# Two attention products cut to 64 and 32 rows of the array: one transpose fewer per head, a second bank for half of the result

## What is computed

```python
def nsa_attend(q, gates, ...):          # 8 query heads, 2 key/value groups
    s = jnp.einsum('bgrtd,bgnd->bgrtn', q, kc) * scale          # 15 compressed blocks
    p_cmp = masked_softmax(s, kc_end[None, :] <= q_pos[:, None])
    o_cmp = jnp.einsum('bgrtn,bgnd->bgrtd', p_cmp, vc)
    ...                                                         # o_sel, o_win in the same way
    return gates[..., 0:1] * o_cmp + gates[..., 1:2] * o_sel + gates[..., 2:3] * o_win
```

## Time and profile before

| what | value |
|---|---|
| runs | 1112.6, 1112.62, 1114.02 us |
| median | 1112.62 us |
| span of the profiled execution, first to last instruction | 1110.9 us |
| PE busy | 1100.0 us (99%) |
| DVE busy | 606.3 us (55%) |
| ACT busy | 419.5 us (38%) |
| mean granted TensorE clock | 0.996 of full speed |

### The profile page before, as it was taken

The page is one execution under the profiler, slowest core; times in us unless marked ns, Lnnn a source line. Parts: engine busy times, 40 slices in busy tenths (PEclk is TensorE's granted clock), DMA queues, the critical chain, the costliest instruction groups (busy, mean ns, idle before and its releaser), DMA issues.

```text
span 1110.9 us, 19312 instructions
## 1 busy us (share of the span) xinstructions
PE 1100.0 (99%) x8020; PEld 1077.8 (97%) x8020; DVE 606.3 (55%) x884; ACT 419.5 (38%) x566; POOL 66.8 (6%) x121
## 2 busy tenths in 40 slices
PE   9999999999999999999999999999999999999996
PEld 7998999999999999999999999999999999999996
DVE  6794443536456667664454467455455454454445
ACT  6733322424335444443333344333333333333332
POOL 0014000000000000001100000000000000002220
PEclk9999999999999999999999999999999999999998
DMA  8556685544444232358888744544544444464342
GB/s 297 196 189 201 228 279 189 179 152 152 168 147 173 83 113 110 114 171 295 288 277 306 257 149 171 171 171 171 171 167 153 168 145 144 147 242 146 148 150 95
DMA packets 64081, 202.03 MB, mean 182 GB/s; under 512 B 6647, under 2 KB 35607, under 8 KB 45831
## 3 DMA queue, kind: packets, MB, share of 16 engines
q1 hardware_dynamic: 58888, 185.68, 48.8%
q0 software_dynamic: 2400, 10.89, 2.8%
q10 hardware_dynamic: 2718, 4.41, 1.1%
HBM read 193.61 MB, written 11.53 MB: 185 GB/s over the span
## 4 chain that ended last, share of the span: by engine, by line
PE 99%; DVE 1%; issue 0%; DVEq 0%
PE bank L1327 27%; PE bank L1328 27%; PE bank L1329 27%; PE bank L1679 1%; PE bank L1360 1%; PE bank L1455 1%; PE bank L1450 1%; PE bank L1429 1%; PE bank L1428 1%; PE bank L1427 1%; PE bank L1594 1%; PE bank L1517 0%; PE bank L1452 0%; PE bank L1685 0%; PE bank L1345 0%; PE bank L1454 0%
## 5 line engine op out<-in xcount | busy, mean ns | idle before, releaser
L536 ACT ACTIVATE w_hi<-raw 128x2048 fp32r<-128x2048 f32 x140 | 268.1, 1915 | 572.2 <-PE bank L1329 479.9
L1327 PE MATMUL bank<-h_hi,w_hi 128*128 128x320 f32 x1536 | 479.7, 312 | 0.0
L1329 PE MATMUL bank<-h_hi,w_lo 128*128 128x320 f32 x1536 | 474.6, 309 | 0.0
L1328 PE MATMUL bank<-h_lo,w_hi 128*128 128x320 f32 x1536 | 474.5, 309 | 0.0
L814 DVE TENSOR_TENSOR w_lo<-raw,w_hi 128x2048 fp32r<-128x2048 f32 x140 | 325.2, 2323 | 186.4 <-ACT w_hi L536 186.2
L1327 PEld LDWEIGHTS bank<-h_hi,w_hi 128*128 128x128 f32 x1536 | 288.4, 188 | 3.9 <-issue 3.5
L1328 PEld LDWEIGHTS bank<-h_lo,w_hi 128*128 128x128 f32 x1536 | 288.5, 188 | 0.4
L1329 PEld LDWEIGHTS bank<-h_hi,w_lo 128*128 128x128 f32 x1536 | 288.4, 188 | 0.0
L1328 PE MATMUL bank<-oz_lo,w_hi 128*128 128x320 f32 x256 | 78.9, 308 | 0.0
L1329 PE MATMUL bank<-oz_hi,w_lo 128*128 128x320 f32 x256 | 78.8, 308 | 0.0
L1327 PE MATMUL bank<-oz_hi,w_hi 128*128 128x320 f32 x256 | 78.8, 308 | 0.0
(11 more groups left out here) (347 smaller groups left out, 1127.5 us busy)
## 6 DMA issues: line engine op xcount, KB each, us to landing
raw<-in_stream SPq DMA_DIRECT2D x140, 1024.0 KB, 5.0
cmp_t<-in_cmp_pages SPq DMA_DIRECT2D x32, 128.0 KB, 4.2
kt_moba<-in_moba_k SPq DMA_DIRECT2D x16, 256.0 KB, 3.6
kt_mem<-in_mem_k SPq DMA_DIRECT2D x8, 512.0 KB, 6.3
vs_moba<-in_moba_v SPq DMA_DIRECT2D x16, 256.0 KB
vs_mem<-in_mem_v SPq DMA_DIRECT2D x8, 512.0 KB
out_win_old<-in_cache_win POOLq DMA_DIRECT2D x8, 512.0 KB, 3.7
raw<-in_stream SPq DMA_DIRECT2D x10, 256.0 KB, 9.9
```

The costliest lines, as they stand in the source:

```text
L536: nc.scalar.activation(w_hi[:, u], raw[:, u], ACT.Copy).then_inc(hi_ready[u], 1)
L1327: nc.tensor.matmul(out[:, 0:n], w_hi[:, u, kb, :], hi[:, kb, :], start=(kb == first), stop=False)
L1328: nc.tensor.matmul(out[:, 0:n], w_hi[:, u, kb, :], lo[:, kb, :], start=False, stop=False)
L1329: mm = nc.tensor.matmul(out[:, 0:n], w_lo[:, u, kb, :], hi[:, kb, :], start=False, stop=(kb == last))
```

## The change

For the prompt: the compressed probabilities of both halves stand side by side in one block `p_c` of 128 columns (the first half in columns 0 to 14, the second in columns 32 to 46), which is transposed once. Of the transposed block rows 0 to 31 and 32 to 63 are multiplied apart, each with a copy of the compressed values on the same rows of `vc_g`: the first half goes on into bank OB, the second into bank P1, which is free after its transposed probabilities are copied out. DVE adds P1 to `o_t` (`compressed_added`, semaphore `c_added`), and TensorE waits for that before it writes P1 again. Two copies of the compressed values are computed per group instead of one.

For the samples: of `vs_new` only rows 0 to 63 are used in the first half of the product and only rows 96 to 127 in the second; the second half of the result goes to bank S2 instead of the second half of OB, and DVE copies the two banks in two instructions.

```diff
-        p_c = at("p_c", [P, 2, P], f32, Z_ + 15 * 4 * TOK)
+        p_c = at("p_c", [P, P], f32, Z_ + 15 * 4 * TOK)
+        p_cq = p_c[:, 0:64].rearrange("p (q n) -> p q n", q=2)
...
                 if i % REP == 0:
-                    nc.vector.tensor_copy(vc_g[0:N_CMP, :], S1[0:N_CMP, 384:512]).then_inc(vc_rdy, 1)
+                    for r in range(0, 64, 32):
+                        nc.vector.tensor_copy(vc_g[r:r + N_CMP, :], S1[r:r + N_CMP, 384:512]).then_inc(vc_rdy, 1)
...
+            def compressed_added(i):
+                dve.wait_ge(o_copied, i + 1)
+                slot = o_t[:, i, P:SEQ]
+                nc.vector.tensor_tensor(slot, slot, P1[:, 0:P], ALU.add).then_inc(c_added, 1)
...
                 z_gated(0, i)
+                compressed_added(i)
                 z_scaled(1, i)
...
-                nc.vector.tensor_copy(o_rows[:].rearrange("p n c -> p (n c)"), OB[:, 0:2 * P]).then_inc(brow_copied, 1)
+                nc.vector.tensor_copy(o_rows[:, 0, :], OB[:, 0:P])
+                nc.vector.tensor_copy(o_rows[:, 1, :], S2[:, 0:P]).then_inc(brow_copied, 1)
...
                 if i % REP == 0:
-                    mm = nc.tensor.matmul(S1[0:N_CMP, 384:512], hid[:, 1, (2 * DEC_BATCH + g) * N_CMP:(2 * DEC_BATCH + g + 1) * N_CMP],
-                                          w_phi2[:, 1, :], start=True, stop=True)
+                    for r in range(0, 64, 32):
+                        mm = nc.tensor.matmul(S1[r:r + N_CMP, 384:512], hid[:, 1, (2 * DEC_BATCH + g) * N_CMP:(2 * DEC_BATCH + g + 1) * N_CMP],
+                                              w_phi2[:, 1, :], start=True, stop=True)
...
-                    nc.tensor.transpose(bk[:, 384:512], p_c[:, n, :], ident[:])
+                    if n:
+                        pe.wait_ge(c_added, i)
+                    if n == 0:
+                        nc.tensor.transpose(bk[:, 384:512], p_c[:], ident[:])
...
-                nc.tensor.matmul(OB[:, 0:SEQ].rearrange("p (q c) -> p q c", q=2), vc_g[:], pt_c, start=False, stop=True)
+                for q in range(2):
+                    rows = slice(32 * q, 32 * q + 32)
+                    nc.tensor.matmul((OB[:, 0:P], P1[:, 0:P])[q], vc_g[rows, :], pt_c[rows, :], start=(q == 1), stop=True)
...
+                for n, r in enumerate(quarter):
+                    nc.tensor.matmul(OB[r, 0:P], ptb_nsa[0:64, 2, r], vs_new[0:64, n * P:(n + 1) * P], start=False, stop=True)
+                for n, r in enumerate(quarter):
+                    nc.tensor.matmul(S2[r, 0:P], ptb_nsa[96:P, 2, r], vs_new[96:P, (4 + n) * P:(5 + n) * P], start=True, stop=False)
```

More of the change, by code:

```diff
@@ L250, in build @@
         (s_ready, vc_rdy, max_rdy, exp_done, p_ready, pt_ready, pt_copied, o_ready, o_copied, z_rdy, z_tanh, z_done, g0_rdy,
-         smp_saved, pt_win_copied) = [sem(n) for n in ("s_ready vc_rdy max_rdy exp_done p_ready pt_ready pt_copied o_ready "
-                                        "o_copied z_rdy z_tanh z_done g0_rdy smp_saved pt_win_copied").split()]
+         smp_saved, pt_win_copied, c_added) = [sem(n) for n in ("s_ready vc_rdy max_rdy exp_done p_ready pt_ready pt_copied o_ready "
+                                        "o_copied z_rdy z_tanh z_done g0_rdy smp_saved pt_win_copied c_added").split()]
         (b_staged, kt_in, vs_in, bs_ready, vcs_ready, vcs_copied, vcs_wr, bmax_rdy, bexp_done, bp_ready, bpt_ready, bpt_copied, brow_ready,
@@ L699, in prompt_exps @@
                 for q in range(2):
-                    softmax_rows(p_c[:, q, 0:N_CMP], q, nmx[:, q:q + 1])
+                    softmax_rows(p_cq[:, q, 0:N_CMP], q, nmx[:, q:q + 1])
                 act.wait_ge(max_rdy, i * 4 + 2)
@@ L731, in _ @@
                 act.wait_ge(pt_ready, i * 3 + 2)
-                nc.scalar.activation(pt_ab[:, 1, :], P1[:], ACT.Copy).then_inc(pt_win_copied, 1)
+                nc.scalar.activation(pt_ab[:, 1, 0:384], P1[:, 0:384], ACT.Copy).then_inc(pt_win_copied, 1)
                 z_tanh_tile(0, i)
@@ L1044, in prompt_softmax @@
                 dve.wait_ge(s_ready, i * 3 + 1)
-                nc.vector.tensor_tensor(p_c[:, 0, 0:N_CMP], S0[:, 0:N_CMP], mask_cmp[:, 0, 0:N_CMP], ALU.add)
-                ch.link(nc.vector.tensor_tensor(p_c[:, 1, 0:N_CMP], S0[:, 384 + N_CMP:384 + 2 * N_CMP], mask_cmp[:, 1, 0:N_CMP], ALU.add))
-                nc.vector.reduce_max(nmx[:, 0:2], p_c[:, :, 0:N_CMP], AX, negate=True).then_inc(max_rdy, 1)
+                nc.vector.tensor_tensor(p_cq[:, 0, 0:N_CMP], S0[:, 0:N_CMP], mask_cmp[:, 0, 0:N_CMP], ALU.add)
+                ch.link(nc.vector.tensor_tensor(p_cq[:, 1, 0:N_CMP], S0[:, 384 + N_CMP:384 + 2 * N_CMP], mask_cmp[:, 1, 0:N_CMP], ALU.add))
+                nc.vector.reduce_max(nmx[:, 0:2], p_cq[:, :, 0:N_CMP], AX, negate=True).then_inc(max_rdy, 1)
                 ch.link(nc.vector.scalar_tensor_tensor(p_sel[:], dist[:, 128:512], slope, S0[:, N_CMP:384 + N_CMP], ALU.mult, ALU.add))
@@ L1074, in scale_p @@
                                                    ALU.mult, ALU.mult)
-                scale_p(p_c[:, 0, 0:N_CMP], 0, 0, 0)
-                scale_p(p_c[:, 1, 0:N_CMP], 1, 1, 0)
+                scale_p(p_cq[:, 0, 0:N_CMP], 0, 0, 0)
+                scale_p(p_cq[:, 1, 0:N_CMP], 1, 1, 0)
                 scale_p(p_sel[:, 0:128], 2, 0, 1)
@@ L1192, in oz_split @@
                                                 ALU.subtract).then_inc(oz_lo_rdy, 1)
-            dve.wait_ge(o_copied, NSA_H)
+            dve.wait_ge(c_added, NSA_H)
             dve.wait_ge(bo_copied, 3 * DEC_BATCH)
@@ L1534, in prompt_values @@
                 pe.wait_ge(pt_win_copied, i + 1)
-                pe.wait_ge(vc_rdy, g + 1)
+                pe.wait_ge(vc_rdy, 2 * g + 2)
                 pe.wait_ge(o_copied, i)
-                pt_sel, pt_win, pt_c = pt_ab[:, 0, :], pt_ab[:, 1, :], pt_ab[:, :, 384:512]
+                pt_sel, pt_win, pt_c = pt_ab[:, 0, :], pt_ab[:, 1, :], pt_ab[:, 0, 384:512]
                 nc.tensor.matmul(OB[:, 0:SEQ], v_rows[:, 0, g * P:(g + 1) * P], pt_sel[:, 0:SEQ], start=True, stop=False)
@@ L1576, in sample_turn @@
                     nc.tensor.transpose(P0[:, m * P:(m + 1) * P], pb[:, m * P:(m + 1) * P], ident[:])
+                if b == 0:
+                    pe.wait_ge(c_added, NSA_H)
                 pe.wait_ge(bp_ready, b * 2 + 2)
@@ L1589, in sample_values @@
                 quarter = [slice(32 * n, 32 * n + 32) for n in range(4)]
-                for m in range(3):
+                for m in range(2):
                     for n, r in enumerate(quarter):
                         vs = (vs_sel, vs_win)[n // 2]
[L1593 to L1600, removed]
+                        nc.tensor.matmul(OB[r, 0:P], ptb_nsa[:, m, r], vs[:, m, n % 2 * P:n % 2 * P + P], start=(m == 0), stop=False)
+                for n, r in enumerate(quarter):
+                    nc.tensor.matmul(OB[r, 0:P], ptb_nsa[0:64, 2, r], vs_new[0:64, n * P:(n + 1) * P], start=False, stop=True)
+                for n, r in enumerate(quarter):
+                    nc.tensor.matmul(S2[r, 0:P], ptb_nsa[96:P, 2, r], vs_new[96:P, (4 + n) * P:(5 + n) * P], start=True, stop=False)
                 for m in range(2):
                     for n, r in enumerate(quarter):
-                        mm = nc.tensor.matmul(OB[r, P:2 * P], ptb_mem[:, m, r], vs_mem[:, m, n * P:(n + 1) * P], start=False, stop=(m == 1))
+                        nc.tensor.matmul(S2[r, 0:P], ptb_moba[:, m, r], vs_moba[:, m, n * P:(n + 1) * P], start=False, stop=False)
+                for m in range(2):
+                    for n, r in enumerate(quarter):
+                        mm = nc.tensor.matmul(S2[r, 0:P], ptb_mem[:, m, r], vs_mem[:, m, n * P:(n + 1) * P], start=False, stop=(m == 1))
                 mm.then_inc(brow_ready, 1)
```

## The result

The changed kernel takes 1117.22 us (median of 5 runs, 1116.8 to 1117.68) against 1112.66 us before (5 runs): ratio 1.0036, 95% interval 1.0025 to 1.0047. It is slower by some 0.4%, above the range of the forecast, which ended at 1116.1. The difference of the two medians is 4.6 us. In later runs, made beside the experiments, before had medians of 1113.5 (19 runs) and 1113.4 us (21 runs), and against these the changed kernel stands 3.7 to 3.8 us higher; the traces say 3.8 us, as follows.

The account below looks back on a forecast made before the run. TensorE, busy 99% and never waiting, was taken as the bound; -0.87 (transposes) - 1.7 (pair) + 1.6 (prompt shape changes) + 0 + 2.4 (sample shape changes) = +1.4 us gave 1114.0 us, range 1109.7 to 1116.1.

Parts of the forecast that it names:

- What bounds the kernel: Whole kernel: TensorE, busy 99%, never waits, so an edit is worth what it adds to or takes from its stream.
- The transposes and the pair: Prompt: 8 of 16 transposes of `p_c` go, -0.87 us; two 32-row products with `vc_g` run together, -1.7 us.
- Rival (c): Prompt: the two 32-row products do not run together, since their 128-column loads follow one another; +3.2 us, 1115.8 us, chance 0.18.
- The price of a change of shape: TensorE: 0.10 us each, 16 in the prompt for +1.6 us, 24 in the samples for +2.4 us.
- (d): Prompt and samples: a change of shape costs 0.13 us instead of 0.10, over 40 changes; +2.6 us, 1115.2 us, chance 0.06.
- the uncovered load of 128 columns: Prompt: upper bound for a change of shape, up to some 0.2 us each if the load stands uncovered; 0.10 was taken.
- Rival (a): Prompt and samples: changes of rows are free; -2.6 us, chance 0.16, or -4.4 us with sample groups together, chance 0.08.
- The 64- and the 32-row groups: Samples: the two groups on `vs_new` do not run together, being of different shapes; no gain taken, bound below -1.8 us.
- Rival (b): Samples: 64- and 32-row groups run together without a change between them, -0.2 us; with the prompt -1.2 us, 1111.4 us, chance 0.12.
- VectorE, the waits, the copies: VectorE's addition, TensorE's wait for `c_added` and the copy of `o_rows` in two pieces are all covered: 0 us.
- The sign forecast for PEld: Weight loads: PEld should show idle time put down to "issue" at each change of shape.

Follow-up runs that it names:

- `prompt_rows_32`: Kernel before, its product of 256 columns with `vc_g` summing over rows 0 to 31 instead of 128, in shape 32x128: 1116.65 us (one run).
- `one_group_64`: Kernel before, the first sample group on `vs_new` summing over rows 0 to 63 instead of 128, in shape 64x32: 1115.53 us (one run).
- `sample_64_64`: Kernel before with only the sample part changed, second group on `vs_new` on rows 64 to 127 instead of 96 to 127: 1114.12 us (one run).
- `best`: Kernel before with one transpose per head, full-row `vc_g` products, and both `vs_new` groups in 64x32 first in `sample_values`: 1111.9 against 1113.39 us, ratio 0.9988.

## Why the prediction was wrong

**What bounds the kernel: right.** TensorE is busy 99%, no new wait of it appears, and every microsecond of the loss is a longer step in its stream.

**The transposes and the pair: right.** The transposes gave 0.11 us per head. The two products of 32 rows run together, as the forecast took from the column strips (measured in strips of 32 columns, so this step to 128 was a choice that came true). Rival (c), that each loads 128 columns and the loads follow one another, is out: one strip alone pays as much for its load as two. The Trainium skill's speed-up of tiles of 32 rows (TensorE: Matmul & The Clock Gate, Measured speedup vs the span model) agrees with that.

**The price of a change of shape: the step that failed.** The forecast took 0.10 us for each of 40 changes. Measured are 0.20 in the prompt and 0.135 in the samples: 16 x 0.20 = 3.2 and 24 x 0.135 = 3.24 instead of 1.6 and 2.4. That is +2.4 us on the forecast's +1.4: 3.8 us, the measured sum of the stages. It stands in every sequence: from the first value product to the scores that follow are 2.18 us after and 1.77 before, where the forecast had 2.1 and 1.8. Of the named cases (d) had this mechanism, a price right in kind and too small, with 0.13 on average where it is 0.16, and a chance of 0.06.

The sum was mis-sized because only the drain was priced. The rows for the rest were there. The earlier trace rows show the product behind the return at 414.59 taking 0.33 us until 414.92, where one of 128 columns takes 0.22; the prediction read the two distances before it and stopped. The lengths of the same line in the trace before say it again, the longest being 0.10 us over the median:

```profile
L1505 PE MATMUL bank<-kv_t,q_t x8: 272/275/377, 414.6 to 475.5; 128*128 128x128 f32 x8
```

The row that the prediction read for leaving the sample products has a second half too. The next row of that timeline before is:

```profile
640.89 0.30 PE L1328 MATMUL bank<-h_lo,w_hi 128*128 128x320 f32 x1
```

The weight product at 640.64 takes 0.25 us until then, where one in the steady stream takes 0.15. So this return costs 0.11 + 0.10 = 0.21 us, and the forecast took the first half for the whole.

The prediction named the uncovered load of 128 columns as the upper bound, up to 0.2 us a change, but left it out of the likeliest sum: 16 changes at 0.2 alone would have taken the forecast to +3.0. It also had no term for what a change costs beyond 0.10 us with weights of 32 columns, 0.024 us of load and 0.01 of drain, 24 x 0.035 = 0.8 us. Together the two give the measured 3.8 us, which is 1116.4 and 0.3 above the range; (d), with 0.03 for every change, came to +2.6. That load of 32 columns could be read before as well: the first pass of the sample products is 0.30 us long and the next one 0.28 (638.75 and 638.88 above).

**Are changes of rows priced like changes of columns?** Yes: 0.09 us of drain into 32x128 and out of it, and with the load 0.135 us into 64x32 and out of it. Rival (a) is out. The Trainium skill's rule that a change of tiling mode drains the engine (TensorEngine Tiling (Array Packing), Key Properties) is borne out for rows by `prompt_rows_32` and `one_group_64`.

**The 64- and the 32-row groups: right.** They did not run together; that they do in one shape is what `sample_64_64` shows. Rival (b) is out for this kernel; where its condition is made true by one shape for both, a sequence costs +0.08 us against before, where (b) had -0.02, again by the loads that it left out.

**VectorE, the waits, the copies: right,** all hidden, the addition with 2.7 us or more, the copies with 1.7 or more. The sign forecast for PEld, idle time put down to "issue", was seen in the samples alone; in the prompt the profile names no cause for it.

The median moved 4.6 us where the stages say 3.8. The start scatters by up to 1.1 us from trace to trace, and against the medians of the later runs of before the changed kernel stands 3.7 to 3.8 us higher. That the rest is scatter is argued from this, not shown by a run of its own.

## What to carry to other kernels

In these runs cutting a product to fewer rows saved nothing in itself: two strips save one product's time, and entering and leaving their shape costs 0.27 us where they and their neighbours have 32 columns of weights and 0.40 us where they have 128, more than the 0.22 us that a product of 128 columns in 32-bit floats takes. It pays where a change of shape stands anyway and the strips can be put beside it (`best`). By these prices it should pay too where three or four products share one visit (an estimate for 128 columns: two products less, 0.44 us, against 0.40); no run tried that. When a switch is priced from a trace, follow the rows behind it until the distances are normal again: part of the price stands in the row after the return.

## What the runs showed of the hardware

- The price of a change of shape has two parts: a drain, 0.09 us in the prompt (`prompt_rows_32`) and 0.11 in the samples (`one_group_64`), and the load of the first weights behind it, which nothing covers: 102 ns for 128 columns, 51 for 64, 24 for 32 (the differences between first and second pass). The product starts with its load and not behind it, and is longer by the load. The Trainium skill, TensorE: Matmul & The Clock Gate, section LDWEIGHTS (loading the stationary operand), gives the time of a load as columns divided by 1.2 in ns. By it 128, 64 and 32 columns are an estimate of 107, 53 and 27 ns; these runs agree to within 5 ns.
- Two row strips of one shape load and multiply together even where both load 128 columns: the pair of L1557 pays one load of 0.10 us, as one strip alone does in `prompt_rows_32`. They write different banks; the same bank was not tried.
- Products in 64x32 and 32x32 on different rows and banks did not overlap: the second group starts 0.35 us behind the first (after), against 0.02 us where both are 64x32 (`sample_64_64`).
